# A hybrid decoder block on one core: the late set of the expert stage becomes 64 tokens with all heads, and the other 64 of the tile share one stationary

## What is computed

```
q = (xn @ wq).reshape(B, S, PEER_HEADS, 2, PEER_HALF)            # 8 heads, halves of 128
s = einsum('bshpd,hpnd->bshpn', q, sub_keys)                     # 128 keys per half
top_v, top_i = top_k(s, 16); cand = top_v[..0,:,None] + top_v[..1,None,:]
cand_v, cand_i = top_k(cand, 16)
experts = i1 * 128 + i2                                          # 16 of 16384 rows per head and token
gates = softmax(cand_v)
act = gelu(einsum('td,tkd->tk', x, u_tab[experts]))              # 128 experts per token
h += einsum('tk,tkd->td', gates * act, v_tab[experts])
out = rms_norm(h, norm_final_g)
```

## Time and profile before

| | us |
|---|---|
| runs | 2796.75, 2794.17, 2790.72; median 2794.17 |
| profiled execution: span, first to last instruction | 2789.1 |
| PE, PEld busy | 2294.5, 2092.9 |
| DVE busy | 2091.1 |
| ACT, POOL busy | 1234.6, 709.7 |
| DMA | 729 MB, mean 262 GB/s |

### The profile page before, as it was taken

The page is one execution under the profiler, slowest core; times in us unless marked ns, Lnnn a source line. Parts: engine busy times, 40 slices in busy tenths (PEclk is TensorE's granted clock), DMA queues, the critical chain, the costliest instruction groups (busy, mean ns, idle before and its releaser), DMA issues. The chain is left out here.

```text
span 2789.1 us, 39739 instructions
## 1 busy us (share of the span) xinstructions
PE 2294.5 (82%) x14809; PEld 2092.9 (75%) x14809; DVE 2091.1 (75%) x2718; ACT 1234.6 (44%) x1872; POOL 709.7 (25%) x394
## 2 busy tenths in 40 slices
PE   7999999999999999999999100013379999999998
PEld 7999999999999888899899000013368878888886
DVE  6785456665645745654459999999977799999996
ACT  4555544444444443443454000149954434444443
POOL 0000000000000100010003786878861233434340
PEclk9999999999999999999999655555589999999999
DMA  7544565555465566564459997999937899999995
GB/s 208 155 152 124 179 182 172 155 152 154 154 201 161 186 188 188 177 193 137 151 189 341 382 399 306 390 403 390 392 147 290 327 415 422 422 422 422 421 414 197
DMA packets 325176, 729.37 MB, mean 262 GB/s; under 512 B 23256, under 2 KB 265136, under 8 KB 267072
## 3 DMA queue, kind: packets, MB, share of 16 engines
q1 hardware_dynamic: 277648, 386.18, 41.5%
q0 software_dynamic: 46912, 340.81, 30.6%
q10 hardware_dynamic: 496, 0.84, 0.1%
HBM read 725.66 MB, written 2.10 MB: 261 GB/s over the span
## 5 line engine op out<-in xcount | busy, mean ns | idle before, releaser
L385 DVE TENSOR_TENSOR b_w_both<-b_raw,b_w_both 128x1024 fp32r<-128x1024 f32 x464 | 569.0, 1244 | 451.9 <-ACT b_w_both L380 450.8
L380 ACT ACTIVATE b_w_both<-b_raw 128x1024 fp32r<-128x1024 f32 x464 | 484.2, 1057 | 571.8 <-PE bank L406 381.8
L406 PE MATMUL bank<-b_act_both,b_w_both 128*128 128x256 f32 x4224 | 515.6, 284 | 1.4 <-ACT b_w_both L380 1.3
L406 PEld LDWEIGHTS bank<-b_act_both,b_w_both 128*128 128x128 f32 x4224 | 509.4, 192 | 3.4 <-ACT b_w_both L380 1.8
L768 POOL DMA_INDIRECT b_u_ring<-in_peer_u,b_idx_all x192 | 416.6, 2170 | 153.0 <-DVE b_dots L2081 76.0
L1202 ACT ACTIVATE b_v_hi<-b_v_raw 128x1024 fp32r<-128x1024 f32 x256 | 271.9, 1062 | 402.0 <-PE bank L1638 308.7
L2081 DVE CUSTOM_DVE_ANT_0 b_u_ring<-b_u_ring,b_xnN 128x2048 f32<-128x2048 f32 x192 | 439.8, 2297 | 0.0
L406 PE MATMUL bank<-b_att_both,b_w_both 128*128 128x256 f32 x3072 | 375.3, 284 | 0.0
L406 PEld LDWEIGHTS bank<-b_att_both,b_w_both 128*128 128x128 f32 x3072 | 371.8, 193 | 0.5 <-issue 0.3
L2133 DVE TENSOR_TENSOR b_v_lo<-b_v_raw,b_v_hi 128x1024 fp32r<-128x1024 f32 x256 | 310.3, 1222 | 67.0 <-ACT b_v_hi L1202 66.1
L1638 PE MATMUL bank<-b_v_hi,b_e_hi 128*128 128x512 f32 x1024 | 317.0, 391 | 0.0
(11 more groups left out here) (321 smaller groups left out, 2381.5 us busy)
## 6 DMA issues: line engine op xcount, KB each, us to landing
b_v_raw<-in_peer_v SPq DMA_DIRECT2D x128, 1024.0 KB
b_raw<-in_w_in SPq DMA_DIRECT2D x208, 512.0 KB, 4.6
b_raw<-in_w_proj_dsa SPq DMA_DIRECT2D x32, 512.0 KB, 4.6
b_raw<-in_w_proj_gla SPq DMA_DIRECT2D x32, 512.0 KB, 3.5
b_raw<-in_w_xk SPq DMA_DIRECT2D x32, 512.0 KB, 4.7
b_raw<-in_w_out SPq DMA_DIRECT2D x32, 512.0 KB, 4.4
b_raw<-in_w_xv SPq DMA_DIRECT2D x32, 512.0 KB, 5.0
b_raw<-in_w_xq SPq DMA_DIRECT2D x32, 512.0 KB, 4.7
```

The costliest lines, as they stand in the source:

```text
L380: act.activation(w_hi[:, q], raw[:, UQ * c + q], ACT.Copy).then_inc(w_high, 1)
L385: dve.tensor_tensor(w_lo[:, q], raw[:, UQ * c + q], w_hi[:, q].bitcast(F32), ALU.subtract).then_inc(w_split, 1)
L406: mm = pe.matmul(proj[c][:, n], lhs, rhs, start=(q == 0 and n == 0 and k == 0 and w is w_hi and x is hi), stop=(q == UQ - 1 and k == UK - ...
```

## The change

The late set is no longer heads 4 to 7 of all 128 tokens of tile 1, but tokens 64 to 127 of that tile with all 8 heads. Its first 64 tokens (`SHARED`) are dense with all heads. So that each group still fills 128 partitions, a group of tile 1 now holds two heads: one head's 64 tokens in partitions 0 to 63, the other's in 64 to 127 (`sims_out`). There are still 16 groups, 12 early and 4 late, 192 early and 128 late gathers. `pack_rows` copies the normed tokens into that order.

The spread weights of the first tile stay; those of the 64 shared tokens are a second array of half the size, made in 16 octets that are now four tokens of full height: four matmuls, one copy. In the value stage high and low weights of the shared tokens stand side by side in one stationary of 128 columns, so that one pair of matmuls with v_hi does both, the low product's rows ending in partitions 64 to 127 of banks 4 to 7: 6 matmuls with v_hi and 4 with v_lo.

The late v rows are added into `hN[:, 1]`, whose upper half holds the residual of the late tokens and whose lower half POOL clears. At the end the two halves are added (the two heads of a group), as are banks 4 to 7's two halves, with copies by ACT across partitions. `late_sum` and its matmuls are gone.

`u_ring` has 6 slots. Four v tiles are held from the start, and late rows have 3 buffers, 4 from row 18, 6 from row 37; they are spaced evenly from step 2 to step 246, and the first two are gathered before the value stage, from within POOL's octet columns. The first two V tiles are asked for as soon as the last dot is done.

```diff
-RING = 8
+RING = 6
+RING_IN_QUERIES = 4
...
-LATE_ALONE = (1, 6, 11, 16, 21, 26, 31)
-LATE_PAIRED = (33, 36, 38, 41, 43, 46, 48, 51, 53, 56, 58)
-TILES_GROW = {48: 24}
-ROWS_GROW = {len(LATE_ALONE): 8, 18: 16, 19: 16}
+LATE_FROM = 2
+LATE_SPAN = STEPS - 10
+ROWS_GROW = {18: 8, 36: 16, 37: 16}
 UNIT = 4
-UNITS = T // UNIT
-HALF = UNITS // 2
+SHARED = P // 2
+HALF = P // UNIT
+OCTETS = SHARED // UNIT
+UNITS = HALF + OCTETS
...
-    spread = sb("spread", [TT, NKEYS, P], RAW)
-
-    late_row = [sb(f"late_row{n}", [D], at) for n, at in enumerate((SML + 4 * C_MASK, RAW, RAW + 72 * K, RAW + 8 * K))]
-    late_sum = sb("late_sum", [D], RAW + 64 * K)
+    xn_late = sb("xn_late", [D], RAW + 120 * K)
+    spread = sb("spread", [NKEYS, P], RAW)
+    spread_shared = sb("spread_shared", [NKEYS, SHARED], RAW + 64 * K)
+
+    late_row = [sb(f"late_row{n}", [D], at) for n, at in enumerate((RAW + 96 * K, RAW + 112 * K, SML + 4 * C_MASK, RAW, RAW + 8 * K,
+                                                                   RAW + 64 * K))]
...
-    e_hi = sb("e_hi", [2, BATCH, T], MRG, F32R)
-    e_lo = sb("e_lo", [2, BATCH, T], MRG + 4 * K, F32R)
-    v_raw = [sb(f"v_raw{n}", [D], at) for n, at in enumerate((HT, WRK + 8 * K, MRG + 8 * K, RAW + 80 * K))]
+    e_parts = sb("e_parts", [2, BATCH, 3 * P], MRG, F32R)
+    E_HI, E_LO, E_SHARED = slice(0, P), slice(P, 2 * P), slice(2 * P, 3 * P)
+    E_SHARED_HI, E_SHARED_LO = slice(2 * P, 2 * P + SHARED), slice(2 * P + SHARED, 3 * P)
+    v_raw = [sb(f"v_raw{n}", [D], at) for n, at in enumerate((HT + 8 * K, RAW + 104 * K, HT, MRG + 8 * K))]
...
+    FIRST_WIDE = PTOP + RING_IN_QUERIES
+    row_slot = [n % RING_IN_QUERIES if n < FIRST_WIDE else (n - FIRST_WIDE + RING_IN_QUERIES) % RING for n in range(EARLY * PTOP)]
+
+    def row_landed(n):
+
+        return u_landed[row_slot[n]], 16 * row_slot[:n + 1].count(row_slot[n])
+
+    def row_before(n):
+
+        same = [m for m in range(n) if row_slot[m] == row_slot[n]]
+        return same[-1] if same else None
...
-    tile_place, tile_back = places(NKEYS, 3, TILES_GROW)
-    row_place, row_back = places(LATE_ROWS, 1, ROWS_GROW)
+    tile_place, tile_back = places(NKEYS, 4, {})
+    row_place, row_back = places(LATE_ROWS, 3, ROWS_GROW)
...
-    def weights_of(b, x):
-
-        return x[:, b % 2].rearrange("p i (a t) -> p i a t", a=TT), spread[:, :, b * BATCH:(b + 1) * BATCH].rearrange(
-            "p a i t -> p i a t")
+    def weights_of(b):
+
+        keys, e = slice(b * BATCH, (b + 1) * BATCH), e_parts[:, b % 2]
+        return ((spread[:, keys], e[:, :, E_HI], e[:, :, E_LO]),
+                (spread_shared[:, keys], e[:, :, E_SHARED_HI], e[:, :, E_SHARED_LO]))
...
+        return [m for m in range(LATE_ROWS) if LATE_FROM + LATE_SPAN * m // LATE_ROWS == n]
...
-        sp.wait_ge(sem("unit_spread"), HALF + 2 * (COLS_KEPT + COLS_ASIDE))
-        sp.wait_ge(sem("seeded"), 1)
+        sp.wait_ge(sem("dotted"), EARLY * PTOP)
         v_rows = a["peer_v"][0]
 
         for j in range(NKEYS):
             if j == 2:
+                sp.wait_ge(sem("unit_spread"), HALF + COLS_KEPT + COLS_ASIDE)
+            if j == 3:
                 sp.wait_ge(sem("unit_spread"), UNITS)
-            if j in TILES_GROW:
-                sp.wait_ge(sem("e_split"), TILES_GROW[j])
-            elif j >= 3:
+            if j >= 4:
                 sp.wait_ge(sem("v_split"), 2 * (j - tile_back[j]) + 2)
             where, count = landed(v_landed, tile_place, j)
...
+        def late_rows(lo, hi):
+
+            pool.wait_ge(sem("dotted"), EARLY * PTOP)
+            for m in range(lo, hi):
+                g, kind, k = LATE[m // (2 * PTOP)], m // PTOP % 2, m % PTOP
+                if m in ROWS_GROW:
+                    pool.wait_ge(sem("e_split"), ROWS_GROW[m])
+                elif m >= 3:
+                    pool.wait_ge(sem("late_used"), m - row_back[m] + 1)
+                where, count = landed(late_landed, row_place, m)
+                pool.indirect_dma_start(late_row[row_place[m]], None, (u_rows, a["peer_v"][0])[kind],
+                                        bass.IndirectOffsetOnAxis(ap=idx_all[:, g * PTOP + k:g * PTOP + k + 1], axis=0)
+                                        ).then_inc(where, 16)
...
             for o in range(COLS_BY_VECTOR, OCTETS):
                 if o == COLS_KEPT + COLS_ASIDE:
+                    late_rows(0, 2)
                     pool.wait_ge(sem("unit_spread"), HALF)
                     pool.wait_ge(sem("routed"), GROUPS)
                 if o >= COLS_KEPT + COLS_ASIDE + COLS_RINGED:
-                    pool.wait_ge(sem("unit_spread"), HALF + 2 * (o - COLS_KEPT - COLS_ASIDE - COLS_RINGED + 1))
+                    pool.wait_ge(sem("unit_spread"), HALF + o - COLS_KEPT - COLS_ASIDE - COLS_RINGED + 1)
                 make_oct_cols(pool, o, "cols_by_pool")
 
         for g in range(EARLY):
             gather_rows(g)
         pool_cols()
 
+        pool.memset(hN[0:SHARED, 1], 0.0).then_inc(sem("late_cleared"), 1)
         pool.wait_ge(sem("rows_by_vector"), OCTETS)
         pool.wait_ge(sem("cols_by_pool"), OCTETS - COLS_BY_VECTOR)
         pool.wait_ge(sem("gate_exped"), GROUPS)
...
+        late_rows(2, LATE_ROWS)
...
+            act.activation(sims[:, j], view[:, :, 0], ACT.Copy, scale=stat[:, 2:3])
+            for n in range(2):
+                src, dst = slice(n * SHARED, (n + 1) * SHARED), slice(c * SHARED, (c + 1) * SHARED)
+                ins = act.activation(sims[dst, PEER_H + 4 * n + i], view[src, :, 1], ACT.Copy, scale=stat[src, 3:4])
             ins.then_inc(sem("sims_ready"), 1)
+
+        def pack_rows():
+
+            act.wait_ge(units_used, unit(END, 0))
+            act.wait_ge(sem("rows_normed"), 1)
+            for n in range(2):
+                act.activation(xn_late[n * SHARED:(n + 1) * SHARED], xnN[SHARED:P, 1], ACT.Copy).then_inc(sem("rows_packed"), 1)
+            act.wait_ge(sem("rows_packed"), 2)
+            act.activation(xnN[SHARED:P, 1], xnN[0:SHARED, 1], ACT.Copy).then_inc(sem("rows_packed"), 1)
...
+            act.activation(spread_shared[:, :, UNIT * o:UNIT * (o + 1)], bank[2 + o % 2].rearrange("p (i t) -> p i t", t=UNIT),
+                           ACT.Copy).then_inc(sem("spread_copied"), 1)
...
+            for w, hi, lo in weights_of(b):
+                ins = act.activation(hi, w, ACT.Copy)
+            ins.then_inc(sem("e_high"), 1)
...
+            if n == STEPS - 4:
+                act.wait_ge(sem("late_used"), LATE_ROWS)
+                act.activation(folded[SHARED:P], hN[0:SHARED, 1], ACT.Copy).then_inc(sem("late_folded"), 1)
+
+
+        for n in range(4):
+            act.wait_ge(sem("v_used"), 2 * NKEYS - 1 + n // 2)
+            act.activation(folded[0:SHARED, n * 512:(n + 1) * 512], bank[4 + n][SHARED:P], ACT.Copy).then_inc(sem("low_folded"), 1)
+            if n % 2:
+                for m in (n - 1, n):
+                    ins = act.activation(hN[:, 0, m * 512:(m + 1) * 512], bank[m], ACT.Square, accum_out=gsum[:, m:m + 1])
...
+                mm = pe.matmul(bank[2 + o % 2][:, m:UNIT * P:UNIT], oct_cols(o)[:, m], oct_rows[:, o % ROWS_HELD, m], start=True,
+                               stop=True)
...
+                part = slice(0, P if n < 4 else SHARED)
+                mm = pe.matmul(bank[n], ident[part], hN[part, n // 4, n % 4 * 512:(n % 4 + 1) * 512], start=True, stop=False,
...
-                for parts, x, done in (((e_hi, e_lo), v_hi[:, v], "v_high_used"), ((e_hi,), v_lo[n % 4], "v_used")):
+                for parts, x, done in (((E_HI, E_LO, E_SHARED), v_hi[:, v], "v_high_used"),
+                                       ((E_SHARED, E_HI), v_lo[n % 4], "v_used")):
                     if done == "v_used":
                         pe.wait_ge(sem("v_split"), b * 4 * BATCH + n + 1)
-                    for t in range(TT):
-                        for e in parts:
-                            for m in range(2):
-                                mm = pe.matmul(bank[4 * t + 2 * v + m], e[:, slot, i, t * P:(t + 1) * P],
-                                               x[:, m * 512:(m + 1) * 512], start=False,
-                                               stop=(last and n >= 4 * BATCH - 2 and done == "v_used"), skip_group_check=True)
+                    for e in parts:
+                        for m in range(2):
+                            mm = pe.matmul(bank[(4 if e is E_SHARED else 0) + 2 * v + m], e_parts[:, slot, i, e],
+                                           x[:, m * 512:(m + 1) * 512], start=False,
+                                           stop=(last and n >= 4 * BATCH - 2 and done == "v_used"), skip_group_check=True)
                     mm.then_inc(sem(done), 1)
...
+            if o == 1:
+                seed(range(2))
         pe.wait_ge(sem("spread_copied"), UNITS)
         seed(range(2, 4)).then_inc(sem("seeded"), 1)
         with pe.Fori(0, NKEYS // (2 * BATCH) - 1) as b:
             values(b)
-        pe.wait_ge(sem("late_used"), LATE_ROWS)
```

(32 more changed lines are left out.)

108 lines of the change are left out of this document (32 added, 76 removed).

## The result

The changed kernel takes 2744.54 us, median of four runs (2743.24 to 2746.17), beside 2793.25 for the kernel before, four runs (2790.72 to 2796.75). The ratio is 0.9824 [0.9811, 0.9837]: 1.8% faster. The forecast was 2732.7 with a range of 2718 to 2756, so it is 11.8 us too low. The profiled execution took 2745.46 us by its own time and 2743.7 by its span.

A forecast was written before the change was run, and what follows sets the result against it. PE bounds the value stage before, transfers after. Stage end 2068.6 + 643 + 1 = 2712.6 against 2777.3 (-64.7), tail +2.2, clock +1: net -61.5, span 2727.6, plus 5.1 kept: 2732.7 us, range 2718 to 2756.

The forecast's parts named there:

- What becomes the bound: Value stage: transfers replace PE as the bound at 627 us, DVE 2% behind, PE waiting about a tenth of the time.
- DVE's 613: Value stage: DVE's v_lo, late multiply-adds, late dots and e_lo work sum to 613 us, under the transfers' 627.
- The stage: Value stage: 620 us of transfers, 3 for landing and use, 20 for nine last steps: 643, plus 1 for three buffers.
- PE's load: Value stage: 10 matmuls per step, 2560 x 0.226 = 579 us, 116 less; PE busy near 90%.
- The rival that the clock falls and stays low: Value stage: PE drops to 1.2 GHz at each step's small wait; 2854 us with a quarter of the steps; chance 0.05.
- The start: First value matmul after the octets moves from 2066.4 to about 2068.6 us, bounds 2066 and 2072.
- Ring: Gather stretch: six slots leave 13.1 us for landings of at most 10.6; cost 0, upper bound 17.
- three buffers: First 36 steps of the value stage: three late buffers; a slot turns in 12.0 to 19.0 us; cost 1, at worst 27.
- tail: From PE's end to the first reduction: 4.2 us instead of 2.0, so +2.2, bounds +1 and +5.
- DVE and the transfers hinder each other: Value stage rival: one late landing stops both; with 3% of 640 lost +19, 2752 us; chance 0.14.
- 392 GB/s: Value stage rival: transfers run at the gather stretch's rate instead of 420, +44, 2776 us; chance 0.05.
- an unfreed PE: Value stage rival: half-height operands cost more per matmul, 0.27 instead of 0.226; no change, 2794 us; chance 0.02.

The follow-up runs named there:

- the three kernels of the middle group: Changed kernel with, singly, twelve matmuls a step: 2789.72 us; late u dots over half their columns: 2735.03; V tiles from the fifth half loaded: 2718.41.
- half-dots kernel: Changed kernel with the 64 dots of late u rows over 1024 of their 2048 columns, octet code untouched: 2735.03 us, one execution.
- last kernel: Changed kernel with early late gathers and POOL's clearing moved behind, late rows over 252 steps, ScalarE's copy after the last v_hi: 2728.49 us, ratio 0.9772.

## Why the prediction was right and where it was wrong

**What becomes the bound: right.** The transfers run at 421 GB/s against the 420 assumed, and the three kernels of the middle group show that they set the length over most of the stage. DVE's 613 bears out too: with transfers to spare and DVE full the stage took 623.0, with its first and last steps.

**The stage: 649.9 against 644, 6 too short.** The forecast had the last late row used 620 + 3 us after the start; its multiply-add began 626.4 and ended 628.8 after it. Some 249 transfers had gone by then, as forecast, but not at the full rate throughout: 358 GB/s in the first 20 us, which were expected at 415 or more, and 349 in the last 27 up to the last late row, where DVE was full. Against 421 that is some 3 and 5 us of transfers. The last nine steps then took 21.1 us against 20. ScalarE's copy of 64 x 2048 did hold the next v_hi:

```profile
2718.23 1.06 ACT L1218 ACTIVATE b_v_hi<-b_v_raw 128x1024 fp32r<-128x1024 f32 x1 [1.21 <-PE bank L1659]
2719.32 1.92 ACT L1290 ACTIVATE b_folded<-b_hN 64x2048 f32<-64x2048 f32 x1
2721.26 1.06 ACT L1218 ACTIVATE b_v_hi<-b_v_raw 128x1024 fp32r<-128x1024 f32 x1
2722.52 1.07 PE L1659 MATMUL bank<-b_v_lo,b_e_parts 128*128 128x512 f32 x4
2724.78 1.07 PE L1659 MATMUL bank<-b_v_lo,b_e_parts 128*128 128x512 f32 x4
```

The v_lo of step 253 starts 3.03 us after that of 252, the ones before it 2.27 apart. But PE's products with v_lo go on every 2.27 us through it, so it cost nothing, as forecast.

**PE's load: near 90% forecast, and the busy share overstates it.** 1566 matmuls of 0.226 are 354 of 400 us, 88%, and PE showed 94% (377.44). It isn't more work: PE meets waits for v_lo, and behind six of the eight gaps of 1.5 to 3.0 us comes a short stretch at 1.2 GHz. Granted clock over 20 us, PE alone (busy, count, clock, DMA share, GB/s), around the waits at 2147 and 2404:

```profile
2120.00:2140.00 20.00, 19.61 (x84) 1.00 1.01 422
2140.00:2160.00 20.00, 16.95 (x67) 0.91 1.01 422
2160.00:2180.00 20.00, 19.57 (x85) 1.00 1.01 422
...
2400.00:2420.00 20.00, 17.00 (x63) 0.83 1.02 424
2420.00:2440.00 20.00, 19.91 (x88) 1.00 1.01 420
```

The transfers stay at 422 to 424 through it, so this cost little or no time. The rival that the clock falls and stays low didn't come. The Trainium skill, "TensorE: Matmul & The Clock Gate", section HAM oscillation, describes a loop that waits for DMA before every burst and loses the clock every time. Here only eight waits of 1.5 us or more stand in the stage; six have a dip behind them, and around the two shown the clock is back at 1.00 in the next 20 us. So the trace shows the fall; a wait before every burst no run here shows.

**The start: the step that failed.** "The start moves from 2066.4 to about 2068.6" was 2080.5, 11.9 of the 16.1 us by which the span was missed. 1.8 of it lies ahead (the last dot at 2036.07 instead of 2033.9 plus the 0.4 kept), which is within what executions of one dense part differ by. The other 10.1 is the octets. The forecast priced POOL's path and took "POOL's pace of 2.3 us an octet" as a cover for everything else. In the half-dots kernel, with the same code, that came true: 34.9 against the 34.3 forecast. Two things were put at nothing. One is that DVE's rows may go two per column of POOL or one, 0.29 or 0.58 us a row; with one, what should be hidden takes as long as what hides it, and every wait of DVE adds to it. The other is POOL's clearing of hN, priced only for late row 2 ("0, at worst +3"): beside slow rows it stood on DVE's path, and moving it gave back 4.8 us (44.4 to 39.6). Between 39.6 and the 34.9 of the half-dots kernel lie another 4.7, the slow rows with what waits for them. These are single executions. With both edits (gathers in POOL's queue, seeds in PE's) and whole rows five of six profiled executions were slow, and without one or both none; why is open. The range kept 2072 as its upper end here; it would have had to be 2080.

**Ring, three buffers, tail: right.** Ring 0 (shown down to five slots). Three buffers: landings took 5.9/24.3/28.1 us against 9.4/14.2/16.4 before, as the queue was full from the start, yet DVE waited for late u rows only 10.2 us in 15 times over the stage; the cost can't be told from the rest of the 6 us that the stage was over. Tail 4.4 against 4.2, and ScalarE's table load now lies beside it: from the first reduction to the end of the span 8.9 us instead of 9.9. The range's high side is added up wrongly: the bounds that it names, 3.4 for the start, 26 for three buffers and 2.8 for the tail, make 32 and not 24, so by its own terms it would have gone to 2765.

**Outside the span: wrong, by luck on the good side.** The 5.1 us kept was the distance of a median of three runs from the span of another execution. In these runs the execution's own time is 1.8 above its span, here and in the last kernel (2730.12 and 2728.3). That took 3.3 us off the error. The sum: start 11.9, stage 5.9, and from the end of PE to the end of the span 1.7 less than forecast (it grew by 1.5; 2.2 and 1 for the clock were kept) are the 16.1 of the span; less 3.3, and less 0.9 as the median lies below the profiled execution, 11.9, the error but for rounding.

**Rivals.** "DVE and the transfers hinder each other" would have given 2752, near the result, but its mechanism isn't there: 68 us less for DVE gave nothing in the stage. 392 GB/s, the low clock and an unfreed PE (1767 matmuls in 400 us are 0.226 each still) fell.

## What to carry to other kernels

Once an engine is relieved, compute the next bounds from rates in a full stretch; transfers at 420 GB/s were good to 1%. Where DVE and POOL run short instructions side by side, a term "hidden under POOL's pace" needs a second price for DVE being slowed by POOL: here it came and went with edits on other engines, and once without any. Before a gain of some us is put down to an edit, compare the stretch that the edit touches: here 9.5 us moved with no edit in their stretch at all. And a last consumer (the late rows) placed ten steps before the end of a stage that transfers set leaves DVE full and the transfers with room at the end: spreading it to the end gave 7.5 us in the stage, one execution beside one, and cost 0.6 in the tail.
